# One-hot operands of the expert-gate scatter laid out with four tokens side by side instead of two

## The reference

```python
expert_idx = take_along_axis(cand_idx, top_pos)      # i1 * 128 + i2, 8 heads x 16 = 128 per token
gates = softmax(top_s)
act = gelu(einsum('td,ted->te', hx, expert_down[expert_idx]))
y   = einsum('te,ted->td', act * gates, expert_up[expert_idx])
```

## Time and profile before

| | |
|---|---|
| time, median of 3 runs | 1972.09 us (1971.73 to 1973.99) |
| profiled execution: its time, its span | 1971.73 us, 1969.9 us |
| TensorE busy | 1945.7 us, 99% of the span |
| VectorE busy | 1370.7 us, 70% |
| ScalarE busy | 757.6 us, 38% |
| GpSimd busy | 1234.1 us, 63% |
| granted TensorE clock, mean | 0.999 |

### The profile page before, as it was taken

One profiled execution on the slowest core, in us unless ns is written; L12 is line 12 of the kernel. 1 busy time (PEld: TensorE's weight loads), 2 busy tenths in 40 slices (PEclk: granted clock), 3 DMA queues, 4 the chain that ended last, 5 costly groups with the idle time before them and its releaser, 6 DMA issues.

```text
span 1969.9 us, 27977 instructions
## 1 busy us (share of the span) xinstructions
PE 1945.7 (99%) x10616; PEld 1701.2 (86%) x10616; DVE 1370.7 (70%) x2345; ACT 757.6 (38%) x1080; POOL 1234.1 (63%) x686
## 2 busy tenths in 40 slices
PE   7999999999999999999999999999999999999998
PEld 6888888888888888999999999999888888888887
DVE  6433333342831479999969989961999999999976
ACT  5322222232552433433344444444333333333362
POOL 5343434353233433799996867766998888888842
PEclk9999999999999999999999999999999999999999
DMA  5222222233323332899997999998999999999931
GB/s 199 86 91 86 91 86 80 92 117 109 86 69 98 99 120 86 306 335 349 368 360 262 406 393 368 392 404 265 362 365 373 360 358 360 367 362 364 358 107 43
DMA packets 171954, 471.95 MB, mean 240 GB/s; under 512 B 13776, under 2 KB 62928, under 8 KB 170064
## 3 DMA queue, kind: packets, MB, share of 16 engines
q1 hardware_dynamic: 58032, 209.04, 30.9%
q0 software_dynamic: 41472, 151.01, 20.4%
q10 hardware_dynamic: 72352, 110.64, 15.7%
HBM read 413.49 MB, written 54.53 MB: 238 GB/s over the span
## 4 chain that ended last, share of the span: by engine, by line
PE 95%; DVE 3%; ACT 1%; issue 0%; DMA 0%; POOL 0%; POOLq 0%; SPq 0%; ACTq 0%; DVEq 0%
PE bank L923 29%; PE bank L925 29%; PE bank L924 29%; PE bank L1177 3%; PE bank L1038 1%; PE bank L1121 1%; PE bank L1106 1%; PE bank L1082 0%; PE bank L1092 0%; DVE bank L1367 0%; DMA xT<-x_cols 0%; PE bank L1129 0%; PE bank L1007 0%; ACT b_hi L596 0%; DVE h_lo L1375 0%
## 5 line engine op out<-in xcount | busy, mean ns | idle before, releaser
L495 POOL TENSOR_TENSOR w_lo<-raw,w_hi 128x1024 fp32r<-128x1024 f32 x390 | 937.4, 2412 | 637.4 <-ACT w_hi L552 633.5
L923 PE MATMUL bank<-h_hi,w_hi 128*128 128x352 f32 (+2 forms) x1560 | 548.8, 352 | 0.0
L925 PE MATMUL bank<-h_hi,w_lo 128*128 128x352 f32 (+2 forms) x1560 | 537.5, 345 | 0.0
L924 PE MATMUL bank<-h_lo,w_hi 128*128 128x352 f32 (+2 forms) x1560 | 537.5, 345 | 0.0
L552 ACT ACTIVATE w_hi<-raw 128x1024 fp32r<-128x1024 f32 x390 | 408.0, 1055 | 321.6 <-DMA raw<-weights 271.4
L924 PEld LDWEIGHTS bank<-h_lo,w_hi 128*128 128x128 f32 x1560 | 294.5, 189 | 19.7
L925 PEld LDWEIGHTS bank<-h_hi,w_lo 128*128 128x128 f32 x1560 | 293.4, 188 | 20.8
L923 PEld LDWEIGHTS bank<-h_hi,w_hi 128*128 128x128 f32 x1560 | 293.0, 188 | 19.4
L1773 DVE TENSOR_TENSOR b_lo<-scr,b_hi 128x384 fp32r<-128x384 f32 x128 | 267.9, 2093 | 49.2 <-ACT b_hi L837 49.1
L925 PE MATMUL bank<-w_hi,b_lo 128*128 128x512 f32 x768 | 298.8, 389 | 0.0
L924 PE MATMUL bank<-w_lo,b_hi 128*128 128x512 f32 x768 | 298.8, 389 | 0.0
(11 more groups left out here) (229 smaller groups left out, 2594.1 us busy)
## 6 DMA issues: line engine op xcount, KB each, us to landing
raw<-weights SPq DMA_DIRECT2D x390, 512.0 KB
act_scratch<-scr ACTq DMA_DIRECT2D x64, 384.0 KB
gate_scratch<-scr ACTq DMA_DIRECT2D x12, 2048.0 KB
scr<-gate_scratch ACTq DMA_DIRECT2D x22, 768.0 KB
scr<-act_scratch ACTq DMA_DIRECT2D x22, 768.0 KB
xT<-gate_scratch ACTq DMA_DIRECT2D x10, 768.0 KB
xT<-act_scratch ACTq DMA_DIRECT2D x10, 768.0 KB
scr<-scr ACTq DMA_DIRECT2D x20, 128.0 KB, 3.9
```

What stands on the lines that cost most here:

```text
L495: return nc.gpsimd.tensor_tensor(w_lo[:, s, :], raw[:, s, :], w_hi[:, s, :].bitcast(F32), ALU.subtract)
L923: nc.tensor.matmul(out, a_hi, c_hi, start=first, stop=False)
L924: nc.tensor.matmul(out, a_hi, c_lo, start=False, stop=False)
L925: return nc.tensor.matmul(out, a_lo, c_hi, start=False, stop=last)
```

## The change

The four tokens of a group become the innermost dimension, of four, in `onehots`, `gated`, the iota and the views of keys and parts. VectorE's two instructions keep their element counts (1,024 and 1,536) and their number. TensorE's 1,152 matmuls keep their number and shape, but for one token the elements of successive keys lie 8 bytes apart. `iota_words` and `iota_T` double, from 128 to 256 words. `keysT` and the parts of the gates are laid out plainly (list after list, part after part) where they were interleaved by groups of four.

```diff
-        with nc.sbuf_tensor("pairs", [P, 4, 2, 2, P, 2], BF16) as onehots:
+        with nc.sbuf_tensor("pairs", [P, 4, 2, P, 4], BF16) as onehots:
-        with nc.sbuf_tensor("gated_pairs", [P, 2, PARTS, 2, P, 2], BF16) as gated_own:
+        with nc.sbuf_tensor("gated_pairs", [P, 2, PARTS, P, 4], BF16) as gated_own:
...
-        keysT = cut(8704, TD).bitcast(BF16).rearrange("p (g n t) -> p g n t", n=2, t=4)
+        keysT = cut(8704, TD).bitcast(BF16).rearrange("p (n t) -> p n t", n=2)
-        iota_words = cut(9600, P)
+        iota_words = cut(9600, 2 * P)
...
-        parts_T = parts_p.bitcast(BF16).rearrange("p (g a b t) -> p g a b t", a=PARTS, b=2, t=2)
-        iota_p = bank[:, 7, S // 2:S // 2 + P]
-        iota_T = iota_p.bitcast(BF16).rearrange("p (k t) -> p k t", t=2)
+        parts_T = parts_p.bitcast(BF16).rearrange("p (a i b c) -> p a i b c", a=PARTS, i=NTG // 2, b=2)
+        iota_p = bank[:, 7, S // 2:S]
+        iota_T = iota_p.bitcast(BF16).rearrange("p (k t) -> p k t", t=4)
...
-                        nc.scalar.activation(keysT[:, :, n, :], bank[:, 2 + n, 0:TD].rearrange("p (g t) -> p g t", t=4),
-                                             ACT.Copy).then_inc(keysT_ready, 1)
+                        nc.scalar.activation(keysT[:, n, :], bank[:, 2 + n, 0:TD], ACT.Copy).then_inc(keysT_ready, 1)
...
-                        ins = nc.tensor.matmul(scattered(q)[:, x, :], onehots[:, q % 4, 0, x // 2, :, x % 2],
-                                               gated[q % 4][:, a, x // 2, :, x % 2], start=a == 0, stop=a == PARTS - 1)
+                        ins = nc.tensor.matmul(scattered(q)[:, x, :], onehots[:, q % 4, 0, :, x],
+                                               gated[q % 4][:, a, :, x], start=a == 0, stop=a == PARTS - 1)
...
-            step(nc.vector.tensor_copy(iota_words.bitcast(BF16).rearrange("p (k t) -> p k t", t=2),
-                                       iota.unsqueeze(2).to_broadcast([P, P, 2])))
+            step(nc.vector.tensor_copy(iota_words.bitcast(BF16).rearrange("p (k t) -> p k t", t=4),
+                                       iota.unsqueeze(2).to_broadcast([P, P, 4])))
...
-                return (keysT[:, 2 * quads * j + q].rearrange("p n (b t) -> p (n b) t", t=2).unsqueeze(2)
-                        .to_broadcast([P, 4, P, 2]))
+                c = 4 * (q % quads)
+                return keys_T[:, :, j, q // quads, c:c + 4].unsqueeze(2).to_broadcast([P, 2, P, 4])
...
-                tt(onehots[:, q % 4].rearrange("p n b k t -> p (n b) k t"), iota_T.unsqueeze(1).to_broadcast([P, 4, P, 2]),
+                tt(onehots[:, q % 4], iota_T.unsqueeze(1).to_broadcast([P, 2, P, 4]),
                    four_keys(j, q), ALU.is_equal).then_inc(oh_compared, 1)
...
-                shape = [P, PARTS, 2, P, 2]
-                tt(gated[q % 4], onehots[:, q % 4, 1].unsqueeze(1).to_broadcast(shape),
-                   parts_T[:, 2 * quads * j + q].unsqueeze(3).to_broadcast(shape), ALU.mult).then_inc(oh_ready, 1)
+                c = 4 * (q % quads)
+                gate = parts_T[:, :, j, q // quads, c:c + 4].unsqueeze(2).to_broadcast([P, PARTS, P, 4])
+                tt(gated[q % 4], onehots[:, q % 4, 1].unsqueeze(1).to_broadcast([P, PARTS, P, 4]), gate,
+                   ALU.mult).then_inc(oh_ready, 1)
```

More of the change, by code:

```diff
@@ L321, in block_program @@
         stage = cut(0, 8192).rearrange("p (b j t) -> p b j t", b=2, t=TG)
-        keysT = cut(8704, TD).bitcast(BF16).rearrange("p (g n t) -> p g n t", n=2, t=4)
-        gated = [gated_own[:, 0], gated_own[:, 1]] + [cut(at, 768).bitcast(BF16).rearrange("p (a b k t) -> p a b k t", a=PARTS, b=2, t=2)
+        keysT = cut(8704, TD).bitcast(BF16).rearrange("p (n t) -> p n t", n=2)
+        gated = [gated_own[:, 0], gated_own[:, 1]] + [cut(at, 768).bitcast(BF16).rearrange("p (a k t) -> p a k t", a=PARTS, t=4)
                                                       for at in (11264, 12032)]
         part_words = cut(9600, PARTS * TD // 2)
-        iota_words = cut(9600, P)
+        iota_words = cut(9600, 2 * P)
         rest = cut(9088, TD)
@@ L430, in scattered @@
             return bank[:, 2 + q % 2, :].rearrange("p (t j) -> p t j", t=4)
+        keys_T = keysT.rearrange("p n (i b c) -> p n i b c", i=NTG // 2, b=2)
         parts_p = bank[:, 6:8, :].rearrange("p a n -> p (a n)")[:, P:P + PARTS * TD // 2]
-        parts_T = parts_p.bitcast(BF16).rearrange("p (g a b t) -> p g a b t", a=PARTS, b=2, t=2)
-        iota_p = bank[:, 7, S // 2:S // 2 + P]
-        iota_T = iota_p.bitcast(BF16).rearrange("p (k t) -> p k t", t=2)
+        parts_T = parts_p.bitcast(BF16).rearrange("p (a i b c) -> p a i b c", a=PARTS, i=NTG // 2, b=2)
+        iota_p = bank[:, 7, S // 2:S]
+        iota_T = iota_p.bitcast(BF16).rearrange("p (k t) -> p k t", t=4)
         idx_p, ids_p = bank[:, 7, 0:P], bank[:, 7, P:P + TOPK]
@@ L1674, in parts_of_gates @@
             def parts_of_gates(at):
[L1676 to L1685, removed]
+                t = slice(at, TD)
+                words = slice(at // 2, TD // 2)
+                rows = part_words.bitcast(BF16).rearrange("p (a t) -> p a t", a=PARTS)
+                of = part_words.rearrange("p (a w) -> p a w", a=PARTS)[:, :, words].bitcast(U32)
+                to = parts_p.rearrange("p (a w) -> p a w", a=PARTS)[:, :, words].bitcast(U32)
+                step(nc.vector.tensor_copy(rows[:, 0, t], gates_s[:, t]))
+                step(tt(rest[:, t], gates_s[:, t], rows[:, 0, t], ALU.subtract))
+                step(nc.vector.tensor_copy(rows[:, 1, t], rest[:, t]))
+                step(tt(rows[:, 2, t], rest[:, t], rows[:, 1, t], ALU.subtract))
                 step(ts(to, of, 0, None, ALU.logical_shift_right))
@@ L1717, in one_hots @@
                     if j == 0 and q == 1:
-                        step(stt(out=ids_extra.rearrange("p (g t) -> p g t", t=4), in0=keysT[:, TZ // 4:, 0, :],
-                                 scalar=float(NKEY), in1=keysT[:, TZ // 4:, 1, :],
+                        step(stt(out=ids_extra, in0=keysT[:, 0, TZ:TD], scalar=float(NKEY), in1=keysT[:, 1, TZ:TD],
                                  op0=ALU.mult, op1=ALU.add))
```

## The result

The changed kernel takes 2037.66 us (median of 4 runs, 2036.92 to 2038.82) against 1972.76 us for the kernel before (median of 4, the three of the time before among them): ratio 1.033, 95% interval 1.0311 to 1.0348, or + 64.9 us. I had said 2030 and a range up to 2037. The profiled execution took 2040.28 us, span 2038.5 us.

What follows compares the result with a forecast made beforehand. TensorE was taken to bound the kernel. Scatter matmuls + 61.4, gap behind groups - 4.3 and iota + 0.3 gave + 57.4 us on 1971.73: 2029.1, against the median 2029.5, said as 2030; whole range 1970 to 2037.

Steps and rivals of the forecast that it cites:

- TensorE bounds, and every added ns of a scatter matmul counts: Whole kernel: TensorE is busy 99% of the span, so savings elsewhere are worth only what it waits for.
- Doubling the pitch doubles the matmul, by 9.6 bytes a ns: Scatter matmuls: streams cover at most 9.6 bytes a ns, so 56.7 ns become 110, + 61.4 us; chance 0.42.
- a delay of one operand is enough: Scatter matmuls: one operand slowed by the 8 byte pitch suffices for the whole + 61.4 us.
- does not acquit the moving operand: Scatter matmuls: bf16 weight loads take 97 ns against 192 for float32, yet the moving operand may still be bound by addresses.
- It is at full rate now; nothing can be gained in it.: Scatter matmul before the change: 56.7 ns for 128 columns, of which 53.3 ns are the columns at 2.4 GHz.
- on top: Scatter matmul before the change: the 3.4 ns it pays beyond 53.3 ns for its 128 columns.
- I take half, 4.3 us: First down matmul behind each of 96 groups: slower scatter matmuls return 0 to 8.6 us; half is taken off.
- can be in time: First down matmul behind a group: its late weights may arrive in time behind slower matmuls, returning 0 to 0.09 us each.
- Together + 0.27 us: VectorE ahead of the first scatter: the doubled iota's cast, + 0.13 us, and its move to PSUM, + 0.13 us.
- No term for the clock: Whole kernel: TensorE's clock was read as granted in full in every slice, so no clock loss was priced.
- VectorE's instructions unchanged: Scatter turns: `compare` and `times_gate` keep 692 and 944 ns, priced at 0; losses hidden up to 25.5 us of slack.
- The pitch is free: Rival for the scatter matmuls: they stay at 56.7 ns, only the iota's + 0.3 us is left, 1972.4 us; chance 0.29.

Runs made afterwards that it cites:

- the two kernels without the wait: Two of the five dots moved from ahead of the first scatter into turn 0: on the kernel before 1970.86 us, on the changed kernel 2034.00 us.

## Why the prediction was right and wrong

- *TensorE bounds, and every added ns of a scatter matmul counts.* Right, shown: + 64.6 us of its busy time, + 64.9 us of time.
- *Doubling the pitch doubles the matmul, by 9.6 bytes a ns.* Right in kind and close in size: + 61.4 us said, + 63.0 measured, 110 ns a matmul said, 1.333 / 12 = 111 measured; and the law held at 6 and at 16 bytes. Alone, the moving operand adds 0.628 us a group (60.3 us, 1.1 less than said), the stationary one 0.036, and both together 0.656. So 2.7 us of the 63.0 come with the stationary operand, which I put at nothing by "a delay of one operand is enough", and they are why the groups came out 1.6 us over the sum. The sentence that a load's quick rate "does not acquit the moving operand" named the right one.
- *"It is at full rate now; nothing can be gained in it."* Nearly: read packed, a matmul takes 54.6 ns for 56.4, so 2 of the 3.4 ns "on top" belong to the 4 byte pitch.
- *"I take half, 4.3 us" of the gap behind a group.* This is the step that failed most: the idea that the next weights "can be in time" behind slower matmuls. 0 came back. The gap is 0.24 us before and 0.25 after, and the load for the second down matmul begins 0.08 to 0.09 us behind the first one's start in both. Without it the sum is 61.7 and the time 1972.8 + 61.7 = 2034.5, inside the range.
- *"Together + 0.27 us" ahead of the first scatter.* The two iota instructions rose by 0.14 us each, as said. But VectorE also came to them 0.46 us later in this trace: the copy at L1666 took 4.41 us for 4.23, and what leads to it began 0.29 us later. The group started 0.73 us later for the 0.27 said. The 0.29 us aren't the change's doing as far as the trace shows: TensorE too came 0.28 us later.
- *No term for the clock.* I read the clock as granted in full in every slice of the trace before, and the sum has no case in which a wait of about 2 us lowers it. In the pair of profiles that cost 1.2 us; the medians can't say how much of it is the change's. The doubling's sum without the gap's return gives 2034.5, so the range left 2.5 us for all else. The groups' 1.6 us over the sum and the 1.6 us that are left for the start and the clock (0.5 and 1.2 in the profiles) carried the time 0.7 us past 2037. The kernel before also stood 0.7 us higher here (1972.76 for 1972.09), which no term of mine covers.
- *VectorE's instructions unchanged.* Right: 692 and 944 ns. By the Trainium skill, "Vector Engine (DVE) Microarchitecture Reference", section 5.1, both layouts qualify for the packed mode; the trace agrees, with the same 692 and 944 ns in both.
- *The pitch is free* (the rival for which the Trainium skill spoke, "SBUF — State Buffer", "Door 1: The DMA port swizzle"). It fell. A line of 16 bytes fits the runs: the cost is the same at pitches of 16 and 24. That two accesses to a line are enough for the full rate doesn't hold for TensorE's moving operand: at 8 bytes two columns share a line, and the matmul takes 109 ns for 56.

## What to carry to other kernels

Where TensorE is the bound, price a strided bf16 operand by the stretch of addresses that its columns cover, not by its elements: up to 4 bytes a column it runs within 2 ns of full rate, beyond that the moving operand pays in proportion (measured at 6, 8 and 16 bytes, no more at 24), and the stationary one a little. So an interleaved layout that serves VectorE's packed mode should keep its runs at two bf16 elements. And a wait of 2 us of a busy TensorE can cost more than itself, as the clock may fall behind it; moving work that isn't needed yet past the first user is cheap.

## What the runs showed that I had not expected

- The cost of the moving operand's pitch is no higher at 24 bytes than at 16: 55, 56, 83, 109, 213, 212 ns a matmul of 128 columns at 2, 4, 6, 8, 16, 24 bytes (at 2 bytes both operands are packed; else the stationary one stays at 4).
- A wait of about 2 us may or may not lower the clock: at waits of 1.95 to 2.4 us it stayed at 1.00 in the profile before and fell in those of the changed kernel and of all eight kernels that altered TensorE's reads (mean granted clock over 1050 to 1062 us: 0.86 in seven of these nine, 0.72 and 0.63 at pitches of 16 and 24 bytes). In the two kernels without the wait it stayed at 1.00. Nothing here shows what decides it.
- A stream that is slowed to 213 ns by its pitch counts as busy, and yet the clock falls to 1.2 GHz behind some of its groups; with the wider gaps that makes 53 us beyond the matmuls' own cost, some 41 of them in down matmuls at the lower clock.
